# A Hyena mixer's long convolutions: transforms at ordinary frequencies, folded twice

## The chip, the cores and the metric

The kernel runs on one core of one Trainium2 chip. The metric is the device time of one execution in microseconds (us). The core has TensorE for matmuls (PE in the profile, its weight loads PEld), VectorE (DVE), ScalarE (ACT), GpSimd (POOL) and DMA queues, which SyncE (SP) and ScalarE issue here. All arithmetic in the part that changes is float32. TensorE's granted clock has two levels, 1.2 and 2.4 GHz, which the profile writes as 0.5 and 1.0.

## The reference, cut to what matters

Two transformer-like blocks are computed. The first has a Hyena mixer of order 2 over 1024 positions and 512 channels; only this mixer changes.

```python
def long_conv(u, hf, bias):
    L = u.shape[1]
    U = jnp.fft.rfft(u, n=2 * L, axis=1)
    y = jnp.fft.irfft(U * hf[None], n=2 * L, axis=1)[:, :L]
    return y + u * bias.astype(jnp.float32)

def hyena_mixer(p, n_rows, conv_w, conv_b, filt, bias):
    L = p.shape[1]
    u = short_conv(p, conv_w, conv_b, n_rows).astype(jnp.float32)
    v, x1, x2 = jnp.split(u, 3, axis=-1)
    hf = hyena_filter_freqs(L, *filt)
    z = x1 * long_conv(v, hf[:, 0], bias[0])
    y = x2 * long_conv(z, hf[:, 1], bias[1])
    return y.astype(p.dtype)
```

`short_conv` is a three-tap convolution along rows of 64 positions. `hyena_filter_freqs` evaluates a small network at 1024 lags, windows and normalises it, and transforms it for both orders.

## The kernel before

The program is a row of stages with a barrier of all engines between them. Two matter.

**The filter stage** (`stage_filter`) makes the spectra of the two filters. TensorE runs 16 transforms (`transform(i)`, two orders, four blocks of 128 frequencies, a cosine and a sine side) of 8 matmuls each, with small matmuls (`tap`) between them. VectorE scales each result out of PSUM (`scale`), GpSimd adds and subtracts the halves (L1386), and SyncE stores them. In its second half VectorE and GpSimd already run three short convolutions and two folds of the next stage.

**The Hyena stage** (`stage_hyena`) runs two long convolutions one after the other, o = 0 and 1. The 512 channels are 4 chunks of 128. Its order is written out by hand for each engine, with semaphores between them.

- *Turn*: GpSimd folds a chunk (lower half of the positions plus and minus the mirrored upper half, `hyena_fold`, L1245 and L1246), TensorE transposes it (`turn`, L1710), ScalarE copies it to `u` (L1646).
- *Forward*: eight steps f, each 8 matmuls of 512 columns against the tables `fwd` (L1728), the first two split into 384 and 128 columns so that they can start before the fourth chunk. For each step VectorE multiplies the two banks with the filter's spectrum (four products, L1842 to L1845), and GpSimd adds and subtracts the products into `p` and `q` (L1601, L1602). The spectrum of each f is loaded by ScalarE's queue.
- *Inverse*: for each chunk c, 16 matmuls of 512 columns against `inv` (L1736), into two banks. ScalarE copies one bank (L1673), VectorE takes sum and difference of the two (L1854, L1855) and multiplies them with the gate x1 or x2 (L1859 to L1865).
- Beside it: VectorE's short convolutions of the other chunks (L1233 to L1235, one each in o = 0 after odd f and after each c); in o = 1 the head of the next stage's mixer (sigmoids, logs, two scans: `head_gates`, `head_keys`, `head_sums`, `head_carried`), the squares (L1682) and their sums by TensorE (L1760).

A float32 matmul stands as two records in the profile, one for each pass. The names `first_raw` and `first_x` in the rows are regions of an earlier stage, reused here: `first_raw` holds raw rows and folds, `first_x` the first mixed chunks and ScalarE's copy.

## Time and profile before

| | us |
|---|---|
| median of 3 runs | 4062.11 (4056.2 to 4063.39) |
| profiled execution, its time | 4056.58 |
| its span | 4054.8 |
| TensorE busy | 3721.8 (92%) |
| VectorE busy | 2566.8 (63%) |
| ScalarE busy | 1900.5 (47%) |
| GpSimd busy | 764.9 (19%) |

The span runs from the first to the last instruction; 1.8 us lie around it. The stages follow each other, so these shares are means over stages with different limits. The filter stage stands at about 470 to 638 us of the span and the Hyena stage at 638.3 to 899.0.

### The profile page before, as it was taken

To read this page: it belongs to the slowest core of one execution; us is meant where nothing else is said; L and a number is where in the kernel's file an instruction comes from. 1 tells how busy PE (TensorE), PEld (TensorE's weight loads), DVE (VectorE), ACT (ScalarE), POOL (GpSimd) and SP (SyncE) were. 2 spreads that over 40 slices of the span, in tenths; PEclk is the share of its full clock that TensorE was granted. 3 is DMA by queue.
4 is the path that set the end of the run, shared out by engine and by line. 5 is a ranking of instruction groups with operands and counts; after the bars stand their busy time and mean duration, and the time that the engine had idled before them with its cause. 6 is when DMAs were issued, how large, how long until landed. Compare 5 with 4: busy or idle time off the path is not lost. (4 is left out here: it accounts for less than half of the span.)

```text
span 4054.8 us, 44136 instructions
## 1 busy us (share of the span) xinstructions
PE 3721.8 (92%) x17357; PEld 2896.9 (71%) x17357; DVE 2566.8 (63%) x2795; ACT 1900.5 (47%) x2499; POOL 764.9 (19%) x591
## 2 busy tenths in 40 slices
PE   7999898986778899999999999999998899999988
PEld 4887644446766487887878787778777577787857
DVE  6445364549856888888888888551375625515753
ACT  5211200047653377777777676451365314514731
POOL 2100034210011011111201011420143224202422
PEclk9999898998898899999999999999999999999999
DMA  5553315120044799999999998443520433435123
GB/s 192 206 182 128 114 68 192 52 85 29 27 167 155 286 378 374 377 368 376 366 372 373 371 378 293 143 137 107 179 91 23 148 123 117 136 108 199 53 94 119
DMA packets 323528, 779.09 MB, mean 192 GB/s; under 512 B 26168, under 2 KB 110003, under 8 KB 323064
## 3 DMA queue, kind: packets, MB, share of 16 engines
q1 hardware_dynamic: 300538, 699.46, 47.4%
q0 software_dynamic: 17856, 66.33, 5.0%
q10 hardware_dynamic: 4928, 10.49, 0.8%
q8 instruction: 138, 2.26, 0.2%
q14 instruction: 68, 0.56, 0.0%
HBM read 664.74 MB, written 111.48 MB: 191 GB/s over the span
## 5 line engine op out<-in xcount | busy, mean ns | idle before, releaser
L3031 DVE TENSOR_TENSOR moe_w_low<-shared_z,moe_w_high 128x2048 fp32r<-128x2048 f32 x256 | 588.1, 2342 | 100.6 <-ACT moe_w_high L2984 100.5
L2984 ACT ACTIVATE moe_w_high<-shared_z 128x2048 fp32r<-128x2048 f32 x256 | 475.7, 1917 | 159.1 <-DMA shared_z<-in_exp_w 152.1
L177 PE MATMUL moe_bank<-moe_w_high,moe_xgT_high 128*128 128x512 f32 x1024 | 403.7, 394 | 4.7 <-POOL moe_xgT_low L2873 4.7
L179 PE MATMUL moe_bank<-moe_w_high,moe_xgT_low 128*128 128x512 f32 x1024 | 401.1, 392 | 0.0
L178 PE MATMUL moe_bank<-moe_w_low,moe_xgT_high 128*128 128x512 f32 x1024 | 400.9, 392 | 0.0
L3031 DVE TENSOR_TENSOR moe_w_low<-moe_w_raw,moe_w_high 128x2048 fp32r<-128x2048 f32 x128 | 287.2, 2284 | 62.9 <-ACT moe_w_high L2984 62.8
L2984 ACT ACTIVATE moe_w_high<-moe_w_raw 128x2048 fp32r<-128x2048 f32 x128 | 238.3, 1911 | 105.3 <-DMA moe_w_raw<-in_exp_w 93.3
L3259 POOL TENSOR_SCALAR layer_att_p<-layer_att_p,layer_att_rinv,layer_att_neg_lam 128x1280 f32<-128x1280 f32 (+1 forms) x72 | 173.3, 2407 | 525.2 <-DVE layer_att_neg_lam L3288 309.7
L3266 DVE TENSOR_REDUCE layer_att_nb<-layer_att_scores 128x1 f32<-128x1280 f32 (+1 forms) x144 | 194.8, 1368 | 86.4 <-PE layer_att_scores L3171 85.5
L177 PE MATMUL layer_front_bank<-layer_front_w_high,layer_front_hT_high 128*128 128x512 f32 (+1 forms) x608 | 230.3, 379 | 7.4 <-POOL layer_front_hT_low L800 7.4
L177 PEld LDWEIGHTS moe_bank<-moe_w_high,moe_xgT_high 128*128 128x128 f32 x1024 | 194.2, 190 | 45.3 <-POOL moe_xgT_low L2873 5.4
L178 PE MATMUL layer_front_bank<-layer_front_w_low,layer_front_hT_high 128*128 128x512 f32 (+1 forms) x608 | 224.2, 369 | 0.0
L179 PE MATMUL layer_front_bank<-layer_front_w_high,layer_front_hT_low 128*128 128x512 f32 (+1 forms) x608 | 223.9, 368 | 0.0
L179 PEld LDWEIGHTS moe_bank<-moe_w_high,moe_xgT_low 128*128 128x128 f32 x1024 | 193.7, 189 | 41.0
L178 PEld LDWEIGHTS moe_bank<-moe_w_low,moe_xgT_high 128*128 128x128 f32 x1024 | 194.3, 190 | 40.0
L3225 ACT ACTIVATE layer_att_p<-layer_att_scores,layer_att_nb 128x1280 f32<-128x1280 f32 (+1 forms) x144 | 177.6, 1233 | 70.2 <-DVE layer_att_nb L3266 70.0
L177 PE MATMUL moe_bank<-moe_w_high,moe_hidT_high 128*128 128x512 f32 x512 | 201.9, 394 | 0.0
L179 PE MATMUL moe_bank<-moe_w_high,moe_hidT_low 128*128 128x512 f32 x512 | 199.4, 389 | 0.0
L178 PE MATMUL moe_bank<-moe_w_low,moe_hidT_high 128*128 128x512 f32 x512 | 199.4, 389 | 0.0
L2872 POOL CAST moe_xgT_high<-moe_xw 128x512 fp32r<-128x512 f32 x32 | 28.0, 874 | 758.6 <-ACT moe_xw L2993 758.6
L177 PE MATMUL front_bank<-front_hT_high,front_w_high 128*128 128x512 f32 (+1 forms) x448 | 168.8, 377 | 0.0
L178 PE MATMUL front_bank<-front_hT_low,front_w_high 128*128 128x512 f32 (+1 forms) x448 | 167.7, 374 | 0.0
(557 smaller groups left out, 8546.2 us busy)
## 6 DMA issues: line engine op xcount, KB each, us to landing
shared_z<-in_exp_w SPq DMA_DIRECT2D x128, 2048.0 KB, 10.0
moe_w_raw<-in_exp_w SPq DMA_DIRECT2D x64, 2048.0 KB, 10.1
shared_z<-in_w_in SPq DMA_DIRECT2D x48, 512.0 KB, 6.3
first_raw<-in_w_in SPq DMA_DIRECT2D x32, 512.0 KB, 7.8
front_vec<-in_ada_w POOLq DMA_DIRECT2D x16, 1024.0 KB, 5.8
late_raw<-in_w_mod SPq DMA_DIRECT2D x8, 2048.0 KB, 8.2
proj_t<-front_out SPq DMA_DIRECT2D x48, 256.0 KB, 2.2
shared_z<-in_w_out SPq DMA_DIRECT2D x12, 1024.0 KB, 6.2
```

Of the source, the lines that this page charges most:

```text
L177: nc.tensor.matmul(out, lhs[0], rhs[0], start=start, stop=False)
L178: nc.tensor.matmul(out, lhs[0], rhs[1], start=False, stop=False)
L179: return nc.tensor.matmul(out, lhs[1], rhs[0], start=False, stop=stop)
L2872: core.pool(pool, nc.gpsimd.tensor_copy(xgT.high[:, c, :], xw[:, c, :]))
L2984: nc.scalar.activation(hi, x, ACT.Copy).then_inc(high, 1)
L3031: nc.vector.tensor_tensor(lo, x, hi.bitcast(F32), ALU.subtract).then_inc(low, 1)
L3225: nc.scalar.activation(p[i % (LAG + 1)][m][:, 0:n], scores[m][:, 0:n], ACT.Exp, bias=nb[:, i, m:m + 1], accum_out=sums[:, i, m:m + 1]).the ...
L3259: nc.gpsimd.tensor_scalar(b, b, rinv[:, i, 1:2], neg_lam[:, :], ALU.mult, ALU.mult).then_inc(scaled, 1)
L3266: nc.vector.tensor_reduce(nb[:, i, m:m + 1], scores[m][:, 0:blocks(i) * P], AX, ALU.max, negate=True).then_inc(bounded, 1)
```

## The change

The transforms move from half-odd to ordinary frequencies. There, even and odd positions can be transformed apart: the results for a frequency and for its mirror are the sum and the difference of the two. So each transform needs half of the matmul work, and more elementwise work joins and splits the parts.

- *Forward*: instead of 8 steps of 8 matmuls, 8 units of 4 (a block f of 128 frequencies, f = 0 to 3, times a cosine or sine side), each into an "even" and an "odd" bank. Frequency 0, the middle one and position 0 need extra terms: one more matmul in two units (cosine side of blocks 0 and 1), three more in one (sine side of block 0). The tables are 1 MB each instead of 2 MB.
- ScalarE copies one bank of each unit (`copy_half`), VectorE takes sum and difference (`part`), makes the eight products of a block (`multiply`; seven short instructions of one partition more in block 0), GpSimd adds and subtracts four times and pairs the `p` tiles with two more, VectorE pairs the `q` tiles (`pair_q`).
- *Inverse*: per chunk 16 matmuls of 256 columns, plus one of 256 and three of one column (`edge`). VectorE writes sum and difference to every other position (`natural`).
- Two short convolutions come before the forward part; the last six have their side terms made by ScalarE (`side_terms`, `conv_with_sides`) and run in o = 0's inverse.
- In the filter stage one transform of each order gets four more matmuls, and TensorE waits there for a small table that is now larger.

```diff
-def hyena_fold(core, n, lo, hi):
+def hyena_fold(core, n, tile, natural):
+
+    half = SEQ // 2
     add, sub = core.hyena_start.fold[n % 2]
-    core.nc.gpsimd.tensor_tensor(add, lo, hi, ALU.add)
-    return core.nc.gpsimd.tensor_tensor(sub, lo, hi, ALU.subtract)
+    lo, hi = tile[:, 1:half], tile[:, SEQ - 1:half:-1] if natural else tile[:, half + 1:SEQ]
+    core.nc.gpsimd.tensor_copy(add[:, 0:1], tile[:, half:half + 1])
+    core.nc.gpsimd.tensor_copy(sub[:, 0:1], tile[:, 0:1])
+    core.nc.gpsimd.tensor_tensor(add[:, 1:half], lo, hi, ALU.add)
+    return core.nc.gpsimd.tensor_tensor(sub[:, 1:half], lo, hi, ALU.subtract)
...
                         for j in range(HF):
                             jj = odd * HF + j
                             last = nc.tensor.matmul(bank[4 + 2 * (i % 2) + odd][:, :], tab[s][:, jj, f * P:(f + 1) * P],
-                                                    fold[o][s][:, jj, :], start=(j == 0), stop=(j == HF - 1))
+                                                    fold[o][s][:, jj, :], start=(j == 0), stop=(j == HF - 1 and not (f == 0 and s == 1 and odd == 0)))
+                        if f == 0 and s == 1 and odd == 0:
+                            for j in range(HF):
+                                last = nc.tensor.matmul(bank[4 + 2 * (i % 2)][:, :], lag0[:, 2:2 + P], fold[o][0][:, j, :],
+                                                        start=False, stop=(j == HF - 1))
                         last.then_inc(spec, 1)
 
+                pe.wait_ge(windows, 16)
...
-                    for f in range(NT):
-                        n = o * NT + f
-                        pool.wait_ge(multiplied, n + 1)
-                        nc.gpsimd.tensor_tensor(pq[0][:, f, :], prod[0][:, :], prod[1][:, :], ALU.add)
-                        nc.gpsimd.tensor_tensor(pq[1][:, f, :], prod[2][:, :], prod[3][:, :],
-                                                ALU.subtract).then_inc(filtered, 1)
...
+                    for f in range(FT):
+                        F = o * FT + f
+                        a, b, e = slots(o, f)
+                        t = term[F % 2]
+                        pool.wait_ge(multiplied, F + 1)
+                        nc.gpsimd.tensor_tensor(G[1][:, a, :], G[1][:, a, :], t[2][:, :], ALU.add)
+                        nc.gpsimd.tensor_tensor(G[1][:, b, :], G[1][:, b, :], t[3][:, :], ALU.add).then_inc(q_summed, 1)
+                        nc.gpsimd.tensor_tensor(G[0][:, a, :], G[0][:, a, :], t[0][:, :], ALU.subtract)
+                        nc.gpsimd.tensor_tensor(G[0][:, b, :], G[0][:, b, :], t[1][:, :], ALU.subtract).then_inc(p_summed, 1)
+                        pool.wait_ge(p_summed, F + 1)
+                        if F:
+                            pool.wait_ge(p_paired, F)
+                        core.pool(pool, nc.gpsimd.tensor_tensor(G[0][:, e, :], G[0][:, a, :], G[0][:, b, :], ALU.add))
+                        nc.gpsimd.tensor_tensor(G[0][:, b, :], G[0][:, a, :], G[0][:, b, :], ALU.subtract).then_inc(p_paired, 1)
...
-                    for s in range(2):
-                        src = u[s] if f < NT // 2 else u[1 - s]
-                        if n == 0:
-                            pe.wait_ge(fwd_table[s], 16)
-                        for j in range(4):
-                            last = nc.tensor.matmul(bank[2 + 2 * (n % 3) + s][:, c0 * P:c1 * P], fwd[s][:, j, f * P:(f + 1) * P],
-                                                    src[:, j, c0 * P:c1 * P], start=(j == 0), stop=(j == 3))
+                    if n < 2:
+                        pe.wait_ge(fwd_table[s], 16 if s else 32)
+                    src = u[s] if f < FT // 2 else u[1 - s]
+                    for half, to in ((0, even), (1, odd)):
+                        for k in range(2):
+                            j = 2 * half + k
+                            more = half == 0 and (f == 0 or f == 1 and s == 0)
+                            last = nc.tensor.matmul(to[:, w], fwd[s][:, j, f * P:(f + 1) * P], src[:, j, w],
+                                                    start=(k == 0), stop=(k == 1 and not more))
+                        if half == 0 and s == 0 and f < FT // 2:
+                            nc.tensor.matmul(to[:, w], fwd[0][0:1, 0, HB:HB + P], u[1][0:1, 0, w], start=False, stop=True)
+                        if half == 0 and s == 1 and f == 0:
+                            for j in range(2):
+                                nc.tensor.matmul(to[:, w], cols[:, 0:P], u[0][:, j, w], start=False, stop=False)
+                            nc.tensor.matmul(to[:, w], cols[0:1, 0:P], u[1][0:1, 0, w], start=False, stop=True)
...
+                    return nc.tensor.matmul(result(n)[r][:, h * HB:(h + 1) * HB], G[k][:, b if h else e, c * P:(c + 1) * P],
+                                            inv[k][:, f, h * HB:(h + 1) * HB], start=(f == 0), stop=(f == FT - 1))
...
-                    else:
-                        if c == 3:
-                            pe.wait_ge(lohi if o == 0 else y_done, CH + 1 - HY_EARLY if o == 0 else 1)
-                        for s in range(2):
-                            for f in range(NT):
-                                last = back_term(n, s, f)
...
+                    for r in range(2):
+                        for h in range(1 if c == 0 else 0, 2):
+                            for f in range(FT):
+                                if f == 2 and h == 0:
+                                    edge(n, r)
+                                last = back_term(n, f, r, h)
...
+                pe.wait_ge(ones_set, 1)
...
+                    dve.wait_ge(half_copied, n + 1)
+                    own, other = (odd if s else even)[:, :], copied[n % 2]
+                    nc.vector.tensor_tensor(pm[f % 2][:, 2 * s, :], own, other, ALU.add)
+                    nc.vector.tensor_tensor(pm[f % 2][:, 2 * s + 1, :], own, other, ALU.subtract).then_inc(released, 1)
...
+                    if F >= 2:
+                        dve.wait_ge(p_summed, F - 1)
...
+                    nc.vector.tensor_tensor(G[1][:, a, :], p, d_, ALU.mult)
+                    nc.vector.tensor_tensor(G[1][:, b, :], p1, d1_, ALU.mult)
+                    nc.vector.tensor_tensor(t[2][:, :], q, c_, ALU.mult)
+                    nc.vector.tensor_tensor(t[3][:, :], q1, c1_, ALU.mult)
+                    nc.vector.tensor_tensor(G[0][:, a, :], p, c_, ALU.mult)
+                    nc.vector.tensor_tensor(G[0][:, b, :], p1, c1_, ALU.mult)
+                    nc.vector.tensor_tensor(t[0][:, :], q, d_, ALU.mult)
+                    last = nc.vector.tensor_tensor(t[1][:, :], q1, d1_, ALU.mult)
+                    if f == 0:
...
+
...
+                    dve.wait_ge(q_summed, F + 1)
+                    if F:
+                        dve.wait_ge(q_paired, F)
+                    step(nc.vector.tensor_tensor(G[1][:, e, :], G[1][:, a, :], G[1][:, b, :], ALU.subtract))
+                    nc.vector.tensor_tensor(G[1][:, b, :], G[1][:, a, :], G[1][:, b, :], ALU.add).then_inc(q_paired, 1)
...
+                    step(nc.vector.tensor_tensor(natural(sm[:, :]), halved(a[:, :]), halved(b), ALU.add))
+                    nc.vector.tensor_tensor(natural(df[:, :]), halved(a[:, :]), halved(b), ALU.subtract)
+                    step(nc.vector.tensor_copy(sm[:, 0:1], b[:, 0:1]))
...
+                    nc.vector.tensor_tensor(to[:, 0:TH], sm[:, :], x[:, 0:TH], ALU.mult)
+                    nc.vector.tensor_tensor(mid, a[:, 0:1], x[:, TH:TH + 1], ALU.mult)
+                    nc.vector.tensor_tensor(rest_of, df[:, 1:TH], x[:, SEQ - 1:TH:-1], ALU.mult
...
                 for i in range(HY_EARLY, CH):
                     conv(i)
                     dve.sem_inc(lohi, 1)
+                for i in range(CH, HELPED[0]):
+                    conv(i)
...
-                        p, q = bank[2 + 2 * (n % 3)][:, :], bank[2 + 2 * (n % 3) + 1][:, :]
...
+                    for f in range(FT):
+                        for s in range(2):
+                            part(UN * o + 2 * f + s)
+                        multiply(o, f)
+                        if f:
+                            pair_q(o, f - 1)
+                    pair_q(o, FT - 1)
...
+                    else:
+                        conv_with_sides(HELPED[0])
```

**VectorE, forward part of o = 0.** `hyena_forward` is the region that holds tables, spectra and the new sums and differences, `hyena_term` holds products, `first_x` ScalarE's copy. Before, two steps f:

```order
L1842 TENSOR_TENSOR hyena_prod<-hyena_bank,hyena_forward 128x512
L1843 TENSOR_TENSOR hyena_prod<-hyena_bank,hyena_forward 128x512
L1844 TENSOR_TENSOR hyena_prod<-hyena_bank,hyena_forward 128x512
L1845 TENSOR_TENSOR hyena_prod<-hyena_bank,hyena_forward 128x512
L1842 TENSOR_TENSOR hyena_prod<-hyena_bank,hyena_forward 128x512
L1843 TENSOR_TENSOR hyena_prod<-hyena_bank,hyena_forward 128x512
L1844 TENSOR_TENSOR hyena_prod<-hyena_bank,hyena_forward 128x512
L1845 TENSOR_TENSOR hyena_prod<-hyena_bank,hyena_forward 128x512
```

Of the change, the rest of one block f with the pairing of the one before it; the four rows L1941, L1942, L1941, L1942 of `part` stand ahead of it, of which the last is shown:

```order
L1942 TENSOR_TENSOR hyena_forward<-hyena_bank,first_x 128x512
L1957 TENSOR_TENSOR hyena_q<-hyena_forward 128x512
L1958 TENSOR_TENSOR hyena_q<-hyena_forward 128x512
L1959 TENSOR_TENSOR hyena_term<-hyena_forward 128x512
L1960 TENSOR_TENSOR hyena_term<-hyena_forward 128x512
L1961 TENSOR_TENSOR hyena_p<-hyena_forward 128x512
L1962 TENSOR_TENSOR hyena_p<-hyena_forward 128x512
L1963 TENSOR_TENSOR hyena_term<-hyena_forward 128x512
L1964 TENSOR_TENSOR hyena_term<-hyena_forward 128x512
L1982 TENSOR_TENSOR hyena_q<-hyena_q 128x512
L1983 TENSOR_TENSOR hyena_q<-hyena_q 128x512
```

Eight instructions with one input in PSUM have become four with one input in PSUM and ten with both inputs in SBUF.

**TensorE, one chunk of the inverse in o = 1.** Of the change (a record here is a whole matmul):

```order
L1841 MATMUL hyena_bank<-hyena_inv_cos,hyena_p 128x256 x2
L1849 MATMUL hyena_bank<-hyena_rest 128x256
L1841 MATMUL hyena_bank<-hyena_inv_sin,hyena_q 128x256 x2
L1841 MATMUL hyena_bank<-hyena_inv_cos,hyena_p 128x256 x2
L1841 MATMUL hyena_bank<-hyena_inv_sin,hyena_q 128x256 x4
L1851 MATMUL hyena_bank<-hyena_cols,hyena_p 128x1
L1852 MATMUL hyena_bank<-hyena_ones,hyena_p 128x1
L1853 MATMUL hyena_bank<-hyena_ones,hyena_rest 128x1
L1841 MATMUL hyena_bank<-hyena_inv_cos,hyena_p 128x256 x2
```

Before, there were 16 rows of 512 columns here. On GpSimd, two rows per step (L1601, L1602), four per two steps, have become six per block:

```order
L1648 TENSOR_TENSOR hyena_q<-hyena_q,hyena_term 128x512
L1649 TENSOR_TENSOR hyena_q<-hyena_q,hyena_term 128x512
L1650 TENSOR_TENSOR hyena_p<-hyena_p,hyena_term 128x512
L1651 TENSOR_TENSOR hyena_p<-hyena_p,hyena_term 128x512
L1655 TENSOR_TENSOR hyena_p<-hyena_p 128x512
L1656 TENSOR_TENSOR hyena_p<-hyena_p 128x512
```

## Rows read from the trace of the kernel before

**Rows 1.** Windows of the Hyena stage: length; busy PE, PEld, DVE, ACT, POOL; clock; DMA.

```profile
638.30:670.50 32.20, 23.82 (x82) 15.41 (x83) 3.51 (x3) 4.61 (x8) 5.08 (x5) 0.70 1.01 379
670.50:727.90 57.40, 57.40 (x147) 26.31 (x147) 39.97 (x44) 0.60 (x1) 25.77 (x16) 1.00 0.36 113
727.90:786.80 58.90, 56.85 (x178) 29.34 (x177) 31.82 (x28) 5.92 (x11) 11.75 (x8) 1.00 0.06 18
786.80:845.50 58.70, 58.70 (x150) 26.89 (x149) 23.72 (x37) 10.14 (x9) 21.12 (x18) 1.00 0.21 67
845.50:899.00 53.50, 47.96 (x156) 26.05 (x155) 21.26 (x24) 22.88 (x27) 0.00 (x0) 0.95 0.10 40
```

**Rows 2.** Timeline of TensorE, Hyena stage: start, duration, instruction, idle before, releaser.

```profile
648.56 5.46 PE L1728 MATMUL hyena_bank<-hyena_forward 128*128 128x384 f32 x8 [3.67 <-DMA hyena_forward<-in_t_fwd_add]
657.11 9.70 PE L1728 MATMUL hyena_bank<-hyena_forward 128*128 128x384 f32 x24 [3.10 <-DMA hyena_forward<-in_t_fwd_sub]
...
737.34 7.03 PE L1736 MATMUL hyena_bank<-hyena_inv_add,hyena_p 128*128 128x512 f32 x16
...
857.01 1.84 PE L1760 MATMUL hyena_bank<-hyena_ones,hyena_mix 128*128 128x1 f32 x16
```

**Rows 3.** Timeline of VectorE, Hyena stage: two products, a gate.

```profile
809.14 0.69 DVE L1842 TENSOR_TENSOR hyena_prod<-hyena_bank,hyena_forward 128x512 f32<-128x512 f32 x1 [4.30 <-PE hyena_bank L1728]
809.75 0.68 DVE L1843 TENSOR_TENSOR hyena_prod<-hyena_bank,hyena_forward 128x512 f32<-128x512 f32 x1
...
861.37 0.68 DVE L1865 TENSOR_TENSOR hyena_mix<-hyena_prod,hyena_mix 128x512 f32<-128x512 f32 x1
```

**Rows 4.** Timelines of GpSimd, then VectorE, filter stage, where both run.

```profile
532.91 3.32 POOL L1386 TENSOR_TENSOR filter_out<-filter_even,filter_odd 128x512 f32<-128x512 f32 x2 [4.91 <-DVE filter_odd L1447]
...
532.75 0.68 DVE L1425 TENSOR_TENSOR filter_abs<-filter_abs 128x512 f32<-128x512 f32 x1
533.46 1.64 DVE L1428 TENSOR_TENSOR filter_acc<-filter_acc,filter_abs 128x512 f32<-128x512 f32 x1
535.13 0.69 DVE L1416 TENSOR_TENSOR filter_sum<-filter_bank,first_raw 128x512 f32<-128x512 f32 x1
```

**Rows 5.** Timelines of VectorE and GpSimd, short convolutions and products' sums.

```profile
643.45 1.27 DVE L1234 SCALAR_TENSOR_TENSOR hyena_mix<-first_raw,col_a,hyena_mix 128x1008 f32<-128x1008 f32 x1
678.10 0.80 DVE L1233 TENSOR_SCALAR hyena_mix<-first_raw,col_a 128x1024 f32<-128x1024 f32 x1
678.94 2.16 DVE L1234 SCALAR_TENSOR_TENSOR hyena_mix<-first_raw,col_a,hyena_mix 128x1008 f32<-128x1008 f32 x1
...
673.08 1.26 POOL L1601 TENSOR_TENSOR hyena_p<-hyena_prod 128x512 f32<-128x512 f32 x1 [24.44 <-DVE hyena_prod L1845]
...
679.99 2.23 POOL L1602 TENSOR_TENSOR hyena_q<-hyena_prod 128x512 f32<-128x512 f32 x1
```

**Rows 6.** Timelines of VectorE, then GpSimd, a later stage, VectorE back to back.

```profile
1586.12 8.22 DVE L3031 TENSOR_TENSOR moe_w_low<-shared_z,moe_w_high 128x2048 fp32r<-128x2048 f32 x3 [1.85 <-ACT moe_w_high L2984]
...
1586.76 3.23 POOL L2873 TENSOR_TENSOR moe_xgT_low<-moe_xw,moe_xgT_high 128x512 fp32r<-128x512 f32 x1
```

**Rows 7.** Timelines of ScalarE and GpSimd, Hyena stage.

```profile
862.09 1.06 ACT L1682 ACTIVATE hyena_mix<-hyena_mix 128x1024 f32<-128x1024 f32 x1 [4.28 <-DVE hyena_mix L1865]
888.25 0.60 ACT L1673 ACTIVATE first_x<-hyena_bank 128x512 f32<-128x512 f32 x1 [5.50 <-PE hyena_bank L1736]
...
639.59 0.10 POOL L1587 MEMSET hyena_ones<- 128x1 f32 x1 [2.03 <-issue]
```

**Rows 8.** Timeline of TensorE, filter stage, second order.

```profile
592.34 7.13 PE L1334 MATMUL filter_bank<-filter_sum,filter_cos 128*128 128x512 f32 x16 [0.35 <-DVE filter_odd L1447]
```

**Rows 9.** Windows of TensorE: length, busy time, granted clock.

```profile
488.00:492.00 4.00, 3.05 (x6) 0.50 0.00 0
...
576.00:580.00 4.00, 4.00 (x7) 0.58 0.19 70
...
915.00:935.00 20.00, 13.25 (x92) 0.83 0.01 4
```

More of the change, by code:

```diff
@@ L1390, in _ @@
                         pool.wait_ge(conv_done, c + 1)
-                        hyena_fold(core, c, *(hyena_half(start.mix[c], h) for h in range(2)))
+                        hyena_fold(core, c, start.mix[c], True)
             @block.vector
@@ L1755, in inverse @@
+                    for r in range(2):
+                        for h in range(1 if c == 0 else 0, 2):
+                            for f in range(FT):
+                                if f == 2 and h == 0:
+                                    edge(n, r)
+                                last = back_term(n, f, r, h)
                     last.then_inc(back, 1)
@@ L1869, in _ @@
+                        if o == 0:
+                            for i in {0: (1, 2), 1: (3, 4), 2: (5,)}.get(c, ()):
+                                conv_with_sides(HELPED[i])
+                        elif c < 2:
+                            head_sums(c)
                 dve.wait_ge(ssq, 1)
@@ L1876, in stage_hyena @@
         for j in range(RSP):
-            core.load[4 + j].close(2 * NT // RSP)
+            core.load[4 + j].close(2 * 2 * FT // RSP)
         for j in range(3):
```

328 lines of the change are left out of this document (222 added, 106 removed).

## The prediction

> **What bounds the kernel now.** I read the stages' windows first, then each engine's timeline inside them. The Hyena stage lasts 260.7 us in five stretches [rows 1]: the start until the first product (32.2), forward o = 0 (57.4, first product to first result), inverse o = 0 (58.9), forward o = 1 (58.7), inverse o = 1 (53.5). In the three stretches from 670.5 to 845.5 TensorE is busy for 173.0 of 175.0 us at a clock of 1.00, and in the forward part VectorE waits for TensorE before a step's products, 4.30 us at 809.14 [rows 3]. A run of 16 records, 8 matmuls of 512 columns, takes 7.03 to the last one's end [rows 2], 0.86 from one start to the next. So a step f costs 6.9 and a chunk of the inverse 13.7. The start is bound by the tables' transfers, with TensorE idle for 3.67 and 3.10 us [rows 2]. In the filter stage TensorE is the bound in both orders' rows of transforms; in the second its only gap is 0.35 us [rows 8].
>
> So matmuls are what the stage pays for, and halving them could save much. The question is what the next bound is.
>
> **The shared resource.** GpSimd's additions take 1.26 us alone (L1601) and 2.23 beside a short convolution of VectorE, which takes 2.16 instead of 1.27 [rows 5]. In the filter stage an addition of VectorE with both inputs in SBUF (L1428) takes 1.64 instead of the 0.68 of its like (L1425), and GpSimd's pair 3.32 instead of 2.5; L1416 beside the same pair, with one input in PSUM, keeps 0.69 [rows 4]. The times fit whole turns: GpSimd's first addition waits for L1425's end (533.43), runs to 534.6, then L1428 runs its 0.55, then GpSimd's second. Back to back it is the same: GpSimd's addition takes 3.23 us, but ends at 1589.99, in the middle of three VectorE instructions that run without idle time until 1594.34 [rows 6]: it got its turn between two of them. So: while GpSimd works, each VectorE instruction with two SBUF inputs can lose about 1.05 us, and one with a PSUM input loses nothing.
>
> The Trainium skill has this as a rule (SBUF — State Buffer, "SBUF: two separate sides"): the shared port pair is an exclusive lock for a whole instruction, not a share of bandwidth, and VectorE takes part with two SBUF inputs. By that rule the sum below stands as it is, and this trace agrees (1.64 against 0.68).
>
> With both engines at full speed in the same walk, the change would save some 32 us more, which is the first rival.
>
> **The change, part by part.** I walked the new order engine by engine with durations of rows. Walked the same way, the order of before gives the stage 260.9 for 260.7 measured.
>
> *Price list.* Matmul of 512 columns 0.86, of 384 0.64, of 256 0.43, of one 0.21 (1.84 for eight [rows 2]), doubled at the lower level of the clock. VectorE, 512 columns: 0.60 from start to start, 0.73 if the next waits for its end (0.69 long [rows 3]). GpSimd 1.22 to 1.26 [rows 5]. ScalarE 0.60 for 512, 1.06 for 1024 columns [rows 7].
>
> *Start, 32.2 becomes 27.5.* TensorE now waits for GpSimd's memset (639.7 [rows 7], against its first transpose at 638.35): +1.4, so forward starts at about 648 to 650, and the smaller tables are there (before, the first landed at 648.5). 17 matmuls of 384 columns are 10.9, plus 2.5 since I let the first 5 us run at the lower level (the stretch had a mean of 0.70 [rows 1]); transposes and copies of the fourth chunk 2.5; five of 128 columns 1.1; the end and ScalarE's copy 0.8: 665.8. Two more short convolutions (0.8 + 1.27 + 1.27 [rows 5]) lie before that and are hidden.
>
> *Forward o = 0, 57.4 becomes 63.1.* TensorE needs only 37 matmuls (31.8 instead of 54.9). But VectorE has 14 instructions per block: 14 x 0.60 = 8.4. Of GpSimd's six (7.5) two lie beside `part`, whose inputs are one in PSUM; each of the other four holds up a VectorE instruction by about 1.03: 4.1. With drains 0.15, a block lasts 12.65. Two steps of before took 13.7: hardly a gain. Added to it: block 0's short instructions (11.2 from its first part to block 1's; I price one partition like 128), block 1 13.8. Then the tail. From the last block's parts: parts 2.4, products 8.1 with three turns lost, GpSimd's last six and VectorE's two pairs 9.6, ten matmuls of 256 columns that wait for the last block 4.5, ScalarE's copy 0.7: 25.4. Sum 11.2 + 13.8 + 12.65 + 25.4 = 63.1. Before, GpSimd's and VectorE's share of a step was smaller and lay under matmuls, the last one's too. ScalarE's `middle` is late too (it stands behind a spectrum load that waits for the last products), which keeps TensorE idle for 18 us, but the last block is later.
>
> *Inverse o = 0, 58.9 becomes 48.2.* TensorE's chunk is 16 x 0.43 + 0.43 + 0.64 = 7.9. VectorE's is longer: `finish` 3.1, two convolutions of which the first meets GpSimd's fold (0.8 + 2.1 + 2.1 [rows 5]) and the second does not (0.8 + 1.2 + 1.2): 11.4. So two chunks at 11.4, one at 8.1 (one convolution), the last finish, and then fold, transposes, copies and 17 matmuls to the first part of o = 1, 17.2. ScalarE's side terms, 1.06 each, are hidden.
>
> *Forward o = 1, 58.7 becomes 65.8*: as before plus 2.7, since TensorE comes to the last block's ten matmuls after idle time and I let them start at the lower level (as at 576, 0.58 after a gap [rows 9]).
>
> *Inverse o = 1, 53.5 becomes 44.2.* The chain through ScalarE and VectorE (gate, square, scale, logs, scan) sets the first interval now, as it did before: 13.9. Then 11.4 and 9.9 instead of 14.0 and 15.6, where ScalarE's copies waited for TensorE (5.50 before the last [rows 7]), and 9 for the end.
>
> Sum: -4.7 + 5.7 - 10.7 + 7.1 - 9.3 = -11.9; the stage takes 248.8.
>
> *Filter stage, +6.5.* Two transforms get four matmuls of 0.86: 2 x 3.43 = 6.9 on TensorE, the bound; the 0.35 gap takes back a little. The small table (66 KB) is issued first and has 3 us until TensorE starts: nothing, at worst 1. VectorE's two additions of one row and GpSimd's copies of one column are hidden by TensorE.
>
> Together -5.4 us.
>
> **Unknown prices.** (1) VectorE writes every other position in `finish`, which no row shows. Lower bound 0: a gate that runs backwards costs 0.68 like any [rows 3]. Upper bound twice the stream, 0.53 for each of 16, which in the walk comes to +11.8. I take 0, as nearest to the backward row. The Trainium skill (VectorE: DVE Perf Modes, "Mode 1×") says that the basic mode takes any stride; by it the price is 0. (2) The clock: 0.50 at 488 between matmuls with gaps, 0.58 at 576 right after a gap, a mean of 0.83 at 915 where a third of the time is idle [rows 9], 1.00 where matmuls are unbroken [rows 1]. If it never fell, -5; if the slow spells were almost twice as long as in my walk, +8. (3) Turns of the port: if GpSimd got only gaps, VectorE would run its eight products through and GpSimd be the bound at about the same 12.7 to 13.4: 0 to +5.
>
> **The rivals.**
> *A, the two engines hardly disturb each other* in these forms: a block falls to 8.9, the stage to 217, the kernel to 4056.6 - 43.7 + 6.5 = 4019. Against it stand rows 4 to 6, three forms on two stages. Chance 0.09.
> *B, slower: TensorE stays at half clock through the inverses.* A chunk then costs 15.5 instead of 11.4, the two waits for the last block 4.3 each: about +33, so 4084. It decides from +13.5 us on. For it: the row at 488, half clock with gaps, and many waits in the new order; against it: in the inverses matmuls come unbroken for 8 us, and such stretches had 1.00 [rows 1]. Partial forms, with a clock or turns worse than taken, get there too. Chance 0.13.
> *C, the gain is eaten*: strided writes or longer spells at the lower clock cost 6 to 13 us, and the time is 4052 to 4061. Chance 0.20.
> *D, as summed*: 0.58.
>
> **How the numbers follow.** The profiled execution took 4056.58 (span 4054.8 and 1.8 around it); -5.4 gives 4051.2. The median of the runs shown is 4062.11, 5.5 above it, and by the same change 4056.7. I predict 4054, between the two. D alone reaches from -14 to +1 around its sum, 4043 to 4062 on both scales. The range 4038 to 4070 takes in C and the milder part of B, and leaves A out. Within 0.2%, 8.1 us, is what a measurement of this kernel can hardly tell from no change. Faster than that: A and somewhat under half of D and C's edge, 0.36. Slower: B and a little of C, 0.14. Same: 0.50.
>
> **What would show it.** Forward block distance near 12.7 us on VectorE, with products of 0.7 and of 1.7 us mixed and `part` always at 0.7; GpSimd's additions at 1.26 and 1.6 to 1.8. TensorE idle in the forward parts, with releasers on VectorE. The stretch from first product to first finish longer than before in both orders, the inverses shorter. `finish` in o = 0 every 11.4 us. Transforms with 12 matmuls in the filter stage. I am wrong if products never exceed 0.7 (A), if L1998 takes over 0.8 (C), or if the granted clock is 0.50 in the inverses (B).

## The result, and the profile after

The changed kernel takes 4065.68 us (median of 20 runs), the kernel before 4057.67 in the same runs: ratio 1.0019 [1.0012, 1.0026], so about 7.7 us slower. In a second comparison (below) the ratio was 1.0027 [1.0017, 1.0038], 11 us. The number lies inside the range 4038 to 4070, and by the first ratio it is still within the 0.2% that the prediction calls no change. But the sum said 5.4 us faster, and that is wrong by 13 to 16 us. That the time fell into the range is owed to the range's width and not to the sum.

The windows of the Hyena stage after, in the five stretches of [rows 1] (start to first `part`, to first `finish`, to first `part` of o = 1, to first `finish` of o = 1, to the next stage); columns as there:

```profile
645.90:677.10 31.20, 26.77 (x84) 16.02 (x84) 10.95 (x10) 5.27 (x9) 6.15 (x9) 0.68 0.82 297
677.10:744.05 66.95, 40.36 (x102) 22.86 (x100) 58.41 (x65) 8.00 (x13) 36.35 (x24) 0.72 0.21 71
744.05:797.60 53.55, 48.68 (x201) 34.65 (x200) 33.45 (x39) 17.04 (x22) 15.45 (x16) 0.90 0.09 30
797.60:863.90 66.30, 40.27 (x102) 21.96 (x100) 59.47 (x66) 15.36 (x18) 38.28 (x26) 0.72 0.18 60
863.90:909.80 45.90, 39.04 (x181) 32.76 (x180) 21.71 (x32) 22.50 (x26) 0.00 (x0) 0.80 0.11 46
```

Against [rows 1] TensorE's clock is what strikes first: 1.00 in the three middle stretches before, now 0.72, 0.90 and 0.72. In the forward parts VectorE is the busy engine, 58.4 of 67.0 us. Finer windows of the same execution show where the clock was at half:

```profile
655.40:667.80 12.40, 12.39 (x21) 5.68 (x21) 6.70 (x6) 0.00 (x0) 2.53 (x3) 0.57 1.04 392
704.30:711.10 6.80, 6.67 (x8) 2.50 (x8) 6.67 (x7) 0.65 (x2) 5.55 (x4) 0.55 0.09 34
728.50:741.00 12.50, 12.50 (x31) 9.36 (x32) 8.50 (x6) 1.93 (x2) 7.30 (x5) 0.50 0.31 109
776.80:788.20 11.40, 11.40 (x21) 5.20 (x21) 1.57 (x5) 0.00 (x0) 2.73 (x4) 0.62 0.00 0
849.00:861.00 12.00, 8.91 (x23) 6.60 (x24) 9.64 (x7) 8.37 (x7) 9.30 (x7) 0.52 0.35 130
883.00:895.00 12.00, 11.91 (x38) 9.15 (x39) 7.20 (x9) 4.21 (x7) 0.00 (x0) 0.57 0.11 45
```

TensorE's timeline says what stood ahead of three of them, a wait each time. The other three stood behind waits too: of 1.60 and 0.69 us before 655.4, of 10.75 before 849.3, and of only 0.98 before 883.1.

```profile
704.34 6.67 PE L1825 MATMUL hyena_bank<-hyena_forward 128*128 128x512 f32 x8 [5.39 <-DVE hyena_forward L1942]
728.49 1.19 PE L1841 MATMUL hyena_bank<-hyena_inv_cos,hyena_p 128*128 128x256 f32 x2 [17.48 <-ACT hyena_rest L1753]
...
774.49 1.53 PE L1805 MATMUL hyena_bank<-ident,first_raw 128*128 128x128 f32 x8 [3.21 <-POOL first_raw L1246]
776.80 2.90 PE L1825 MATMUL hyena_bank<-hyena_forward 128*128 128x384 f32 x4 [0.78 <-ACT hyena_forward L1699]
```

Two matmuls of 384 columns (x4 at 776.80) take 2.90, where full speed gives 1.5. Between the slow spells the inverses run at full clock: the mean is 1.00 from 744 to 772 us. VectorE and GpSimd in a forward block (timelines; the answers to [rows 3] and [rows 5]):

```profile
704.80 0.67 DVE L1942 TENSOR_TENSOR hyena_forward<-hyena_bank,first_x 128x512 f32<-128x512 f32 x1
705.61 1.60 DVE L1957 TENSOR_TENSOR hyena_q<-hyena_forward 128x512 f32<-128x512 f32 x1
707.14 1.75 DVE L1958 TENSOR_TENSOR hyena_q<-hyena_forward 128x512 f32<-128x512 f32 x1
708.81 1.75 DVE L1959 TENSOR_TENSOR hyena_term<-hyena_forward 128x512 f32<-128x512 f32 x1
710.48 0.68 DVE L1960 TENSOR_TENSOR hyena_term<-hyena_forward 128x512 f32<-128x512 f32 x1
...
704.17 1.27 POOL L1650 TENSOR_TENSOR hyena_p<-hyena_p,hyena_term 128x512 f32<-128x512 f32 x1
705.40 1.26 POOL L1651 TENSOR_TENSOR hyena_p<-hyena_p,hyena_term 128x512 f32<-128x512 f32 x1
706.74 1.59 POOL L1655 TENSOR_TENSOR hyena_p<-hyena_p 128x512 f32<-128x512 f32 x1
708.41 1.60 POOL L1656 TENSOR_TENSOR hyena_p<-hyena_p 128x512 f32<-128x512 f32 x1
```

`part` (L1942), with an input in PSUM, keeps 0.67 beside GpSimd's additions. The products, with two inputs in SBUF, take 1.6 to 1.75 as long as GpSimd works and 0.68 when it has stopped. These are the turns as predicted. The strided writes of `finish` cost nothing:

```profile
755.66 0.69 DVE L1998 TENSOR_TENSOR hyena_term<-hyena_bank,first_x 128x512 f32<-128x512 f32 x1
756.38 0.69 DVE L1999 TENSOR_TENSOR hyena_term<-hyena_bank,first_x 128x512 f32<-128x512 f32 x1
```

The five stretches of every kernel of this study, read from the same rows of each timeline (SyncE's first issue of the stage, first `part`, first `finish`, SyncE's first issue of the next stage), one profiled execution each, and the ratio to the kernel before:

| kernel | start | fwd 0 | inv 0 | fwd 1 | inv 1 | stage | ratio to before |
|---|---|---|---|---|---|---|---|
| before | 32.2 | 57.4 | 58.9 | 58.7 | 53.5 | 260.7 | 1 |
| predicted | 27.5 | 63.1 | 48.2 | 65.8 | 44.2 | 248.8 | |
| changed | 31.2 | 67.0 | 53.6 | 66.3 | 45.9 | 263.9 | 1.0019 [1.0012, 1.0026] |
| changed, again | 28.5 | 65.9 | 53.6 | 66.1 | 45.9 | 259.9 | 1.0027 [1.0017, 1.0038] |
| memset wait late | 28.1 | 66.4 | 53.5 | 66.1 | 45.9 | 260.0 | 1.0016 [1.0007, 1.0025] |
| filter without 2 x 4 matmuls | 30.7 | 66.5 | 53.5 | 66.1 | 45.9 | 262.8 | 1.0001 [0.999, 1.0011] |
| all waits filled | 28.5 | 66.7 | 49.1 | 65.2 | 45.9 | 255.4 | 1.0012 [1.0002, 1.0022] |
| additions of one column | 31.1 | 50.8 | 53.4 | 50.2 | 45.9 | 231.4 | 0.9932 [0.9912, 0.9952] |
| middle copies early | 29.2 | 66.0 | 53.5 | 66.1 | 45.9 | 260.7 | 1.0027 [1.0016, 1.0038] |
| one wait filled | 29.5 | 65.9 | 49.1 | 66.6 | 45.9 | 256.9 | 1.0013 [1.0005, 1.0022] |
| parts in PSUM | 27.7 | 56.7 | 53.6 | 56.0 | 45.9 | 239.9 | 0.9977 [0.9968, 0.9987] |
| the same, turn filled, memset late | 28.1 | 56.2 | 49.1 | 56.3 | 45.9 | 235.7 | 0.9961 [0.9948, 0.9975] |
| and inverse waits filled | 28.2 | 54.1 | 49.1 | 54.3 | 45.9 | 231.6 | 0.9952 [0.9938, 0.9966] |
| and start filled instead | 25.6 | 55.8 | 49.1 | 56.4 | 45.9 | 232.7 | 0.9958 [0.9944, 0.9971] |
| all of these | 28.3 | 54.1 | 49.1 | 55.9 | 45.9 | 233.2 | 0.9944 [0.9928, 0.996] |

Ahead of the stage, the filter stage (SyncE's first issue to the next stage's) goes from 167.2 to 174.2, and to 171.9 in the second profile. After the stage the code is the same. The first profile lies 10.8 us later than before at the Hyena stage's end and 18.7 later at the program's end; VectorE's instructions set side by side show that nearly all of the other 8 arise at 2100 to 2550 us (10.9 at 2116, 16.8 at 2397, 18.4 at 2535), while expert weights stream in, where nothing was changed. The second is 4.7 later at the stage's end and 6.0 at the program's.

### The profile page after: what moved, and what is told of

Same layout as the page of the kernel before. It is cut to its first block and busy times, and to the rows that moved or that the text cites. A ratio compares the mean times of both kernels' runs of the same rounds, so it can differ in the third digit from the quotient of the medians.

```text
span 4073.5 us, 44284 instructions
## 1 busy us (share of the span) xinstructions
PE 3679.4 (90%) x17333; PEld 2907.8 (71%) x17333; DVE 2636.2 (65%) x2873; ACT 1923.9 (47%) x2531; POOL 814.4 (20%) x623
## 5 line engine op out<-in xcount | busy, mean ns | idle before, releaser
L3071 POOL CAST moe_xgT_high<-moe_xw 128x512 fp32r<-128x512 f32 x32 | 36.9, 1155 | 762.3 <-ACT moe_xw L3192 762.3
```

Source lines behind the costliest of these rows:

```text
L3071: core.pool(pool, nc.gpsimd.tensor_copy(xgT.high[:, c, :], xw[:, c, :]))
```

## The experiments

Five questions were put to the chip: the memset wait, the filter stage's matmuls, the clock, the turns of the shared port, and the late copies. The two theories behind them were: (1) the turns cost what the sum said, and TensorE's clock after waits costs much more than it said; (2) the clock's slow spells lie beside other work, and the loss has another cause (the turns worse than priced, a late copy, the filter stage).

**The memset wait.**

```diff
-                pe.wait_ge(ones_set, 1)
                 for c in range(3):
                     turn(c)
...
                     if o == 0:
                         pe.wait_ge(table, 32)
+                        pe.wait_ge(ones_set, 1)
```

> TensorE's wait for GpSimd's memset moves from the start of the Hyena stage to just before the first inverse. Theory (the clock is what the prediction mis-sized; the early wait is a small part): the first transposes start 1.3 us earlier (they stood at 647.35, 1.4 after SyncE's first issue at 645.92; GpSimd's memset at 647.19), and the kernel is 1 to 2 us faster than the changed one, still slower than before by about 6. Rival (the start is bound by the raw rows or the tables): the transposes start earlier, forward does not, 0 us.

Measured 1.0016 [1.0007, 1.0025]. The start is 28.1 us, against 31.2 and 28.5 of the two profiles of the changed kernel. A gain of 1 us would fit and can't be told from none by these intervals; the rival isn't excluded.

**The filter stage.** In `transform` the four extra matmuls go, and with them their condition in `stop`.

> Leaves out, in the filter stage, the four extra matmuls that one transform of each order got (so the middle frequency of the spectra is wrong). Both theories: two times 3.43 us of TensorE, so the filter stage falls by 6.9 of its 7.6 us and the kernel by 6.5 to 7.5 against the changed kernel. If it falls by much less, those matmuls lay beside other work and the 7.6 us come from the wait for the small table or from GpSimd's additional copies.

Measured 1.0001 [0.999, 1.0011], that is 7.3 us less than the changed kernel by its first ratio (0.0018 of 4056) and 10.5 by its second. The filter stage takes 165.8 instead of 174.2 and 171.9, 6.1 to 8.4 less. The term of 6.9 us fits. Without these matmuls the change would have been no loss, but no gain either.

**TensorE kept at work in all waits.** A helper issues matmuls that nobody reads:

```diff
+                def warm(to, moving, count):
+                    for _ in range(count):
+                        nc.tensor.matmul(to[:, :], core.ident[:, :], moving, start=True, stop=True)
...
+                        warm(bank[1], fwd[1][:, 0, :], {5: 4, 7: 5 - o}.get(i, 0))
                         pe.wait_ge(released, n - 2)
...
                         for f in range(FT):
+                            warm(bank[1], inv[0][:, 0, :], [[17, 0, 0, 1], [2, 3, 12, 3]][o][f])
                             pe.wait_ge(p_paired, FT * o + f + 1)
...
                             turn(CH + 1)
+                            pe.wait_ge(lohi, CH - HY_EARLY + 2)
+                            warm(bank[3], inv[0][:, 0, :], 3)
                             turn(CH + 2)
...
                         if o and c:
+                            warm(bank[1], inv[0][:, 0, :], 1)
                             square_sums(c - 1)
```

> TensorE does matmuls of 512 columns into a bank that nobody reads while it would wait in the Hyena stage: 4 and 5 before forward units 5 and 7 (4 and 4 in o = 1), 17 before the inverse of o = 0, 2, 3, 12 and 3 before the blocks of o = 1's first chunk, 3 before the last turn, 1 before each row of square sums. The computed result is the same. Theory 1 (the half clock after each wait is what the sum lacked): the granted clock in the stretches after these waits (0.50 after the wait of 17.5 us, 0.62 at the forward part of o = 1, 0.52 and 0.57 in o = 1's inverse) rises to 0.9 or more, and the kernel gets 8 to 16 us faster than the changed one, so 0 to 8 us faster than before. Theory 2 (the wait for VectorE and GpSimd sets the end in these places, and TensorE's slow matmuls lie beside them): the clock rises, but the time falls by under 3 us, or rises by what the fillers overrun.

Measured 1.0012 [1.0002, 1.0022]: 3 us less than the changed kernel by its first ratio and 6 by its second, below the 8 to 16 of theory 1. The table splits it: inverse 0 falls by 4.5, forward 1 by 1.0, forward 0 and inverse 1 not at all. So the slow spell at 883 to 895 us was indeed beside other work (theory 2 for that place), and in forward 0 the fillers brought nothing. TensorE's timeline there:

```profile
705.12 14.75 PE L1839 MATMUL hyena_bank<-hyena_inv_cos,ident 128*128 128x512 f32 x34
724.07 0.67 PE L1846 MATMUL hyena_bank<-hyena_inv_cos,hyena_p 128*128 128x256 f32 x2 [4.19 <-ACT hyena_rest L1753]
...
728.12 1.22 PE L1846 MATMUL hyena_bank<-hyena_inv_sin,hyena_q 128*128 128x256 f32 x2
...
731.44 1.91 PE L1839 MATMUL hyena_bank<-hyena_inv_cos,ident 128*128 128x512 f32 x2
733.14 1.06 PE L1846 MATMUL hyena_bank<-hyena_inv_sin,hyena_q 128*128 128x256 f32 x2
```

The fillers ended 4.19 us before the wait did. The first matmuls behind that rest still took 0.67, but from 725.1 us on a matmul of 256 columns took 1.06 to 1.22 instead of 0.6, and the single filler at 731.44 then took 1.9 us itself, right where the last block was awaited. Here the fillers that ended early bought nothing, and the one that ran at half clock cost its time.

**One wait filled.** Of these edits only the three fillers before the last turn.

> Of the fillers only three matmuls of 512 columns before the last turn, in the 3.2 us in which TensorE waits for GpSimd's fold ahead of o = 1. Theory (this is where the half clock costs most): the forward part of o = 1 that follows runs at a clock near 1.00 instead of 0.62 in its first 11.4 us, the inverse stretch of o = 0 falls from 53.6 to 49 or 50 us, as it did with all fillers (49.1), and everything else stays; the kernel 4 to 4.5 us faster than the changed one. Rival (the fillers in the other waits were needed for it too): the clock stays near 0.6 there and the stretch above 52.

Measured 1.0013 [1.0005, 1.0022]. The window of this kernel from the last turn into the forward part of o = 1, as long as 776.80:788.20 above:

```profile
773.00:784.40 11.40, 10.62 (x31) 5.19 (x30) 2.72 (x6) 0.74 (x2) 2.73 (x4) 1.00 0.00 0
```

And TensorE's timeline there:

```profile
768.79 2.74 PE L1838 MATMUL hyena_bank<-hyena_inv_cos,ident 128*128 128x512 f32 x6
771.88 1.23 PE L1805 MATMUL hyena_bank<-ident,first_raw 128*128 128x128 f32 x8 [0.35 <-POOL first_raw L1246]
773.89 1.53 PE L1825 MATMUL hyena_bank<-hyena_forward 128*128 128x384 f32 x4 [0.78 <-ACT hyena_forward L1699]
```

Clock 1.00 instead of 0.62, the first two matmuls of 384 columns 1.53 instead of 2.90, inverse 0 at 49.1 instead of 53.6, everything else as it was. Three matmuls of 0.86 us, in a wait of 3.2, give back 4.5 us in the trace, as expected. The ratio, 2 to 6 us below the changed kernel's two, goes with it, but the intervals overlap. This is theory 1, shown by the trace at one place.

**GpSimd's additions on one column.**

> GpSimd's six additions and subtractions of each block work on one column instead of 512 (so sums of products are left out; one memset is added at the start). Theory (turns of the shared port, as predicted): no product of VectorE exceeds 0.7, the block distance falls from 12.75 to 8.5 to 8.9 us, the time from first part to first finish falls by 14 to 16 us in each order (4 per block and the additions at the end), the kernel by 27 to 33. Rival (VectorE's long products have another cause, such as its own writes or ScalarE's copies): products of 1.75 us remain and the block distance stays above 12.

Measured 0.9932 [0.9912, 0.9952], four runs. Against the changed kernel that is 35 to 39 us less by the ratios, 31 by the medians (4034.88 and 4065.68), and 28.5 to 32.5 by the stage in the traces: the expected 27 to 33, or a little more. VectorE's timeline:

```profile
691.27 0.69 DVE L1958 TENSOR_TENSOR hyena_q<-hyena_forward 128x512 f32<-128x512 f32 x1
691.88 0.68 DVE L1959 TENSOR_TENSOR hyena_q<-hyena_forward 128x512 f32<-128x512 f32 x1
692.48 0.68 DVE L1960 TENSOR_TENSOR hyena_term<-hyena_forward 128x512 f32<-128x512 f32 x1
...
697.43 0.68 DVE L1942 TENSOR_TENSOR hyena_forward<-hyena_bank,first_x 128x512 f32<-128x512 f32 x1
```

All products 0.7, and a block every 8.7 us (688.76, 697.43, 706.20) instead of 12.75 to 13.9. So the turns cost 4.0 to 5.2 per block. The other 7 of the 16 us per forward part lie behind the last block's first `part`: its own turns, and GpSimd's additions, which nothing waits for any more. This experiment takes away the additions together with the turns; the one with parts in PSUM below separates the two.

**The middle copies early.** ScalarE's `load_spectrum(FT + 1)` moves behind its two copies.

> ScalarE sends off the last spectrum load of o = 0 after its two small copies for the middle frequency instead of before them, so TensorE no longer waits 17.5 us for these copies in o = 0 (they stood behind the load's wait for the last products). Theory as in the prediction (the last block is later anyway): the first chunk's blocks 0 to 2 are done about 12 us earlier, the wait moves to the last block, and the first finish comes 0 to 2 us earlier, less what TensorE's clock takes back after the new wait; the kernel 0 to 2 us faster than the changed one. Rival (that wait is the cause of the loss): first finish 5 us or more earlier.

Measured 1.0027 [1.0016, 1.0038], forward 0 at 66.0. TensorE's wait of 17.5 us splits into 5.5, 9.4 and 2.6, and the first `finish` comes no earlier. That conspicuous wait was never on the path.

**Parts in PSUM.** The same work on the same engines; the sums and differences of `part` lie in PSUM, so that the products have one input there. For that the units take turns over eight banks instead of six, and TensorE waits for products where it waited for `part`.

```diff
-                    nc.vector.tensor_tensor(pm[f % 2][:, 2 * s, :], own, other, ALU.add)
-                    nc.vector.tensor_tensor(pm[f % 2][:, 2 * s + 1, :], own, other, ALU.subtract).then_inc(released, 1)
+                    nc.vector.tensor_tensor((even if s else odd)[:, :], own, other, ALU.add)
+                    nc.vector.tensor_tensor(own, own, other, ALU.subtract).then_inc(released, 1)
...
-                    p, p1, q, q1 = (pm[f % 2][:, i, :] for i in range(4))
+                    p1, p = (b_[:, :] for b_ in unit(UN * o + 2 * f)[3:])
+                    q, q1 = (b_[:, :] for b_ in unit(UN * o + 2 * f + 1)[3:])
...
-            b = 2 + 2 * (i % 3)
+            b = ((2, 4, 6, 0), (4, 6, 2, 0))[o][i % 4]
...
-                    if i >= 3:
-                        pe.wait_ge(released, n - 2)
+                    if i >= 4:
+                        pe.wait_ge(multiplied if s else freed, FT * o + (i - 4) // 2 + 1)
```

> VectorE writes sum and difference of each unit (its part) back into the unit's own two PSUM banks instead of SBUF, so its eight products read one input from PSUM; for that the units take turns over all 8 banks. Same result, same number of instructions on each engine. Theory (turns of the shared port between VectorE's instructions with two SBUF inputs and GpSimd's additions cost the forward parts 4 us per block): products take 0.7 each, GpSimd's additions 1.26 except beside the pairing of q; block distance 9.5 to 10.5 instead of 12.75; the walk gives 228 to 233 for the stage instead of 263.9 measured (248.7 in the same walk), so the kernel is 15 to 25 us faster than the changed one and 8 to 18 faster than before. What can take it back: TensorE's two units per block (6.9 at full clock) now wait for the products of the block before last, and at half clock they would take 14 and be the bound. Rival (VectorE's long products are due to GpSimd's load alone or to bank or write conflicts, not to where the inputs lie): products of 1.75 remain, block distance above 12, no gain.

Measured 0.9977 [0.9968, 0.9987]: 9 us faster than before and 17 to 20 faster than the changed kernel. VectorE, then GpSimd at the same time, timelines:

```profile
697.36 0.68 DVE L1958 TENSOR_TENSOR hyena_q<-hyena_bank,hyena_forward 128x512 f32<-128x512 f32 x1
697.95 0.68 DVE L1959 TENSOR_TENSOR hyena_term<-hyena_bank,hyena_forward 128x512 f32<-128x512 f32 x1
...
702.25 1.64 DVE L1983 TENSOR_TENSOR hyena_q<-hyena_q 128x512 f32<-128x512 f32 x1
...
697.88 1.27 POOL L1654 TENSOR_TENSOR hyena_p<-hyena_p 128x512 f32<-128x512 f32 x1
```

Products 0.68 beside an addition of 1.27 on GpSimd; only the pairing of q, whose inputs both lie in SBUF, still waits its turn (1.64). The block distance is 9.67, the forward parts 56.7 and 56.0. The rival is out: what counts is where the inputs lie. TensorE's two units per block were not the bound (it waited 0.9 to 2.5 us before them).

**Together, and more fillers.**

> The kernel with parts in PSUM, together with the two small edits: TensorE's wait for the memset only before the first inverse, and three fillers before the last turn. If the three effects add (parts in PSUM 17 us, fillers before the turn 4.5, the memset 1.2), the stage takes 233 to 236 us instead of 239.9 and the kernel is 20 to 25 us faster than the changed one, 12 to 17 faster than before. If the clock before o = 1 was part of what the PSUM parts gave, it is no better than these alone.

Measured 0.9961 [0.9948, 0.9975], 15.8 us faster than before; the stage takes 235.7, inside the 233 to 236 of effects that add.

> The same, and fillers in the waits of the first inverse chunk of each order (13 before block 0 and 2 before block 3 in o = 0; 1, 9 and 3 before blocks 1, 2 and 3 in o = 1). Theory (the half clock costs where TensorE's ten matmuls of 256 columns after the last block are awaited by VectorE): they take 4.3 us instead of 5.7, the first finish comes 1.5 to 3 us earlier in each order, the kernel another 2 to 5 us faster. Rival (fillers end late or the clock falls all the same in the rest of the wait): within 1 us of the kernel without them.

Measured 0.9952 [0.9938, 0.9966]. The times can't be told from the kernel without these fillers, the traces can: forward 0 and 1 are 2.1 and 2.0 us shorter. Here the fillers ended 0.33 us before the wait, and TensorE's matmuls behind it ran at full speed (timeline of this kernel):

```profile
714.10 0.67 PE L1844 MATMUL hyena_bank<-hyena_inv_cos,hyena_p 128*128 128x256 f32 x2 [0.33 <-ACT hyena_rest L1752]
714.61 0.59 PE L1844 MATMUL hyena_bank<-hyena_inv_sin,hyena_q 128*128 128x256 f32 x2
```

The same matmuls in the kernel without these fillers:

```profile
713.46 1.19 PE L1844 MATMUL hyena_bank<-hyena_inv_cos,hyena_p 128*128 128x256 f32 x2 [14.16 <-ACT hyena_rest L1752]
714.45 1.06 PE L1844 MATMUL hyena_bank<-hyena_inv_sin,hyena_q 128*128 128x256 f32 x2
```

> As the second kernel before this one (PSUM parts, late memset wait, three fillers before the last turn), and at the stage's start seven more fillers of 128 columns: four before the third transpose group and three before the first forward unit, where TensorE waits 1.6 and 0.7 us. Theory (the start's spread of 28.1 to 31.2 us among kernels with the same instructions there comes from when the clock rises, and unbroken work makes it rise sooner): the first part comes 27 us or less after the stage's start, 1 to 3 us earlier. Rival (the clock rises when it does, whatever lies in these two gaps): no difference beyond the spread.

Measured 0.9958 [0.9944, 0.9971], the time unchanged within the intervals; in the trace the start is 25.6 instead of 28.1. TensorE's first forward matmuls took 1.53 instead of 2.93, and it now waits for tables.

> All edits that helped: parts in PSUM, late memset wait, fillers before the last turn, in the start's two gaps and in the waits of the first inverse chunks. If they add: start 25.6, forward parts 54.2 each, inverses 49.1 and 45.9, stage about 229 us; 20 to 24 us faster than before (ratio 0.994 to 0.995). If the fillers of the start only shift where the clock falls later, no better than without them (0.9952).

Measured 0.9944 [0.9928, 0.996], 22.7 us faster than before, the best of the kernels that compute the whole result. The time is as expected, but the stage took 233.2 and not 229: the start was 28.3, with the same fillers, and the forward part of o = 1 55.9 instead of 54.3. TensorE's first forward matmuls with the start fillers alone:

```profile
652.82 1.53 PE L1824 MATMUL hyena_bank<-hyena_forward 128*128 128x384 f32 x4 [0.47 <-DMA hyena_cols<-in_t_hy_cols]
```

And with all fillers:

```profile
654.93 2.90 PE L1824 MATMUL hyena_bank<-hyena_forward 128*128 128x384 f32 x4 [2.55 <-DMA hyena_cols<-in_t_hy_cols]
```

The small table landed 2 us later in this execution, TensorE idled 2.55 instead of 0.47, and the clock was at half again. In the forward part of o = 1 the fillers before the last block ended too early:

```profile
825.35 1.22 PE L1844 MATMUL hyena_bank<-hyena_inv_sin,hyena_q 128*128 128x256 f32 x2 [2.27 <-POOL hyena_p L1655]
```

In the kernel without start fillers the same matmul stood behind a rest of 1.21 us and took 0.70. Fillers sized for a wait hold only while what stands before and after them keeps its time.

> The changed kernel itself once more, beside the version with all edits: its ratio to before (1.0019 the first time) and the spread of the stage's start, whose instructions no earlier experiment without start fillers touched but for the memset wait (28.1 to 31.2 us among them). Theory (the clock rises at a moment that differs from run to run): start between 28.5 and 31.2, the four other stretches within 1 us of 67.0, 53.6, 66.3 and 45.9. If the start is 31.2 again, the spread belongs to the kernels and not to the run.

Start 28.5; the forward part of o = 0 is 1.1 us shorter than in the first profile, just over the expected 1, the rest within 0.2. So the start's spread, 28.1 to 31.2 with one set of instructions behind the first transposes, belongs to the execution and not to the kernel.

## Why the prediction was wrong

The forecast said faster and the kernel is slower. Step by step, with the mean of the two profiles of the changed kernel:

- *Turns of the port*: right in mechanism and size. Forecast block distances 13.8 and 12.65, measured 13.9 and 12.75. Rival A is excluded by the trace. The experiment that makes its premise true gives a stage of 231 us, where A said 217: the same 13 or 14 us too low, since the terms below are in its sum too. The rule of the Trainium skill (SBUF — State Buffer, "SBUF: two separate sides"), on which nothing of the sum hung, is borne out by 0.68 against 1.75 for the same product from PSUM and from SBUF.
- *Inverses*: the pace of `finish` 11.6 (forecast 11.4), then 8.3; in o = 1, 14.0, 11.65 and 10.1 (13.9, 11.4, 9.9). Right. What was wrong stands at their end: the 17.2 us from the last `finish` of o = 0 to the first part of o = 1 took 22.1.
- **The clock, the step that failed.** The sum priced half clock at the start (2.5) and for the last block of o = 1 (2.7), about 5 us in all, and put every other place at nothing, without a reason: not even the ten matmuls after the last block of o = 0 were priced, though the text itself has TensorE idle for 18 us shortly before them. The text said that if the spells were almost twice as long the sum would be 8 higher, and left that to rival C. Measured by undoing it: 4.5 us in the 17.2 before o = 1 (priced at 0), 2.1 at the end of forward 0 (priced at 0 in a tail of 25.4, which took 27.2 and 28.3), 2.0 at the end of forward 1 (priced 2.7), and 2.6 at the start in the one execution where it worked (priced 2.5). Together 11 instead of 5. The last three are measured in kernels with parts in PSUM, one trace each; that they are as large in the changed kernel is an inference. The walk had the clock come back after 5 us of unbroken matmuls; the windows at 728.50 and 776.80 show it below 0.65 over 11 to 12.5 us of them. The rows of before had a warning that I read too mildly: 0.50 at 488 and 0.58 at 576 [rows 9] are both behind gaps between matmuls, such as the new order makes in many places, while the 1.00 of [rows 1] was taken in stretches whose longest gap was 0.83 us.
- *Small terms*: block 0 takes 12.0, not 11.2, in each order; the end of the last inverse 10.1, not 9 (before it took 10.0, from 888.95 to 898.96, so this was simply misread); the start is 29.8 on average for 27.5, of which the memset wait may be 1. Together about 5. Another 2 us lie in distances and tails that are 0.1 to 0.4 longer each than in the walk.
- *Filter stage*: 6.5 forecast; 7.0 and 4.7 in the profiles, 7.3 or 10.5 by the experiment in times. Right, as far as this can be told.
- *Strided writes*: 0, as taken (0.69). *The late middle copies*: off the path, as said.

By stretches: start +2.3, forward 0 +3.3, inverse 0 +5.4, forward 1 +0.4, inverse 1 +1.7, filter -0.7 against the forecast, in all 12.4, where the two ratios ask for 13 and 16. The clock is 6 of it: half of the miss and its largest term, and by itself enough to turn 5.4 faster into no gain. The small terms made it a loss.

Rival B named the mechanism and the wrong extent (half clock through the inverses, 33 us). What came true is C's other half, "longer spells at the lower clock", beside small terms nearly all of one sign. C's time was miscalculated: 6 to 13 us on the sum's 4051.2 give 4057 to 4064, and on the medians' scale 4063 to 4070, not the 4052 to 4061 that it names. The measured 4065.68 lies in that; the miss of 13 to 16 us is C's upper end and a little more. That the sum of -5 was the small difference of terms of 5 to 11 us each, with an unknown of 8 on one side, should have put "slower" well above 0.14.

Left open: whether the memset wait costs 1 us or nothing, and why the clock rises sooner in one execution than in another (the start varies by 3 us, the filter stage between 171.9 and 174.3); both are below what these runs can part. With one profile for each kernel, differences under 1 us in the table, and any in its column for the start, say little.

## What to carry to other kernels

Halving TensorE's work moves a stage onto the engines that join and split the halves: price their instructions with both inputs' places, since VectorE's with two SBUF inputs and GpSimd's take turns, and let intermediate results stay in PSUM where banks allow (here 17 to 20 us of 4060). When a change turns unbroken matmuls into bursts, look at every burst behind a wait and charge it the half clock where VectorE awaits it, 2 to 5 us each here. Fillers paid only there, and only where they lasted nearly until the wait ended: behind rests of 0.33, 0.35 and 1.21 us the clock stayed full, behind those of 2.27, 2.55 and 4.19 it did not. The longest wait of an engine (17.5 us here) can be worth nothing while one of 3.2 us costs 4.5.

## What the hardware showed beside this

- VectorE writes into PSUM, in place too, in the same 0.66 to 0.70 us per 512 columns as into SBUF, and keeps clear of the turns.
- An instruction of VectorE on one partition costs as much as on 128: L1968, 1 x 512, takes 0.68. A memset of 1 x 512 takes 0.48.
- Beside unbroken products of VectorE (1.75 each, one per 1.67 us from 692.24 to 698.93) GpSimd's additions take 1.59 to 1.72 and come one per 1.7 to 1.8 us: the two engines alternate, instruction by instruction.
- The granted clock can fall behind a short rest too: after 0.98 us of idle time before 883.09 it was 0.57 over the next 12 us, in which TensorE was busy for 11.9. The slow spell cost nothing, since the inverse of o = 1 took 45.9 us with and without it.
- How soon the clock rises at the stage's start varied between executions with the same instructions, by up to 3 us of a start of 28 to 31.
